# mLSTM mixing in a fused model block: column sums in four groups at once with a fold, and the mixing a half slot later

## What is computed

```python
scores = einsum('jd,sd->js', q, k) * w            # w: exp of gate sums, masked
den    = sum(scores, axis=-1)                     # "denominators"
out    = (scores @ v) / maximum(abs(den), exp(-m))
hh     = out[forward] + out[backward]
mu     = mean(hh, axis=-1)
var    = mean((hh - mu) ** 2, axis=-1)            # "variances"
y      = (hh - mu) * rsqrt(var + eps) * ln_w * sigmoid(o) ... * silu(z)
```

## Time and profile before

| what | us |
|---|---|
| median of 3 runs | 1283.39 (1282.34 to 1285.04) |
| the profiled execution, its own time | 1281.4 |
| its span, first to last instruction | 1279.6 |
| TensorE busy | 1204.3 |
| VectorE busy | 865.3 |
| ScalarE busy | 603.3 |
| GpSimd busy | 198.5 |

### The profile page before, as it was taken

One profiled execution on the slowest core, in us unless ns is written; L12 is line 12 of the kernel. 1 busy time (PEld: TensorE's weight loads), 2 busy tenths in 40 slices (PEclk: granted clock), 3 DMA queues, 4 the chain that ended last, 5 costly groups with the idle time before them and its releaser, 6 DMA issues.

```text
span 1279.6 us, 22795 instructions
## 1 busy us (share of the span) xinstructions
PE 1204.3 (94%) x9284; PEld 1118.9 (87%) x9284; DVE 865.3 (68%) x1355; ACT 603.3 (47%) x920; POOL 198.5 (16%) x145
## 2 busy tenths in 40 slices
PE   5799899999999999989999999999989789999996
PEld 2477698978888999989999899999978778999996
DVE  2889834458688867564368887665478996876644
ACT  3423354556656455651253354453455555445433
POOL 1334100000000000002000412210006951122000
PEclk9799999999999999999999999999999899999999
DMA  9565312214222355540345435545523213455550
GB/s 387 234 266 219 143 44 107 82 67 165 99 99 99 109 188 211 197 167 31 104 171 190 163 134 197 194 169 194 196 101 129 103 60 139 168 194 194 171 195 33
DMA packets 27475, 195.58 MB, mean 153 GB/s; under 512 B 3192, under 2 KB 3328, under 8 KB 3968
## 3 DMA queue, kind: packets, MB, share of 16 engines
q1 hardware_dynamic: 26496, 191.90, 41.5%
q10 hardware_dynamic: 896, 2.50, 0.5%
HBM read 193.33 MB, written 1.05 MB: 152 GB/s over the span
## 4 chain that ended last, share of the span: by engine, by line
PE 81%; DVE 10%; ACT 4%; issue 1%; DMA 0%; POOL 0%; ACTq 0%; DVEq 0%
PE ps L444 24%; PE ps L445 23%; PE ps L446 23%; DVE acc L2212 3%; PE ps L469 3%; PE ps L727 2%; DVE w_lo L1593 2%; PE ps L553 1%; PE ps L715 1%; PE ps L484 1%; DVE xconv L1697 1%; ACT w_hi L1010 1%; ACT x_hi L1306 1%; PE ps L612 1%; PE ps L777 1%
## 5 line engine op out<-in xcount | busy, mean ns | idle before, releaser
L1593 DVE TENSOR_TENSOR w_lo<-ring,w_hi 128x1024 fp32r<-128x1024 f32 x282 | 349.0, 1256 | 173.6 <-ACT w_hi L1010 166.6
L1010 ACT ACTIVATE w_hi<-ring 128x1024 fp32r<-128x1024 f32 x304 | 315.1, 1054 | 305.5 <-PE ps L446 220.5
L444 PE MATMUL ps<-x_hi,w_hi 128*128 128x258 f32 (+1 forms) x1216 | 346.5, 285 | 7.6 <-DVE x_lo L1943 4.1
L445 PE MATMUL ps<-x_lo,w_hi 128*128 128x258 f32 (+1 forms) x1216 | 344.0, 283 | 0.0
L446 PE MATMUL ps<-x_hi,w_lo 128*128 128x258 f32 (+1 forms) x1216 | 343.7, 283 | 0.0
L444 PEld LDWEIGHTS ps<-x_hi,w_hi 128*128 128x128 f32 x1216 | 231.0, 190 | 11.0 <-issue 10.8
L445 PEld LDWEIGHTS ps<-x_lo,w_hi 128*128 128x128 f32 x1216 | 231.1, 190 | 0.1
L446 PEld LDWEIGHTS ps<-x_hi,w_lo 128*128 128x128 f32 x1216 | 230.7, 190 | 0.0
L444 PE MATMUL ps<-g_hi,w_hi 128*128 128x256 f32 x608 | 171.0, 281 | 3.1 <-POOL g_lo L1537 1.7
L446 PE MATMUL ps<-g_hi,w_lo 128*128 128x256 f32 x608 | 170.3, 280 | 0.0
L445 PE MATMUL ps<-g_lo,w_hi 128*128 128x256 f32 x608 | 170.3, 280 | 0.0
(11 more groups left out here) (348 smaller groups left out, 1959.3 us busy)
## 6 DMA issues: line engine op xcount, KB each, us to landing
ring<-in_weights SPq DMA_DIRECT2D x156, 1024.0 KB, 4.8
o_sb<-in_weights SPq DMA_DIRECT2D x10, 1024.0 KB, 7.1
ada_room<-in_weights SPq DMA_DIRECT2D x10, 1024.0 KB, 7.0
V<-in_weights SPq DMA_DIRECT2D x3, 1024.0 KB, 22.6
dft<-in_dft ACTq DMA_DIRECT2D x1, 1026.0 KB, 7.0
X<-in_x SPq DMA_DIRECT2D x1, 1024.0 KB, 5.2
ctx_room<-in_ctx SPq DMA_DIRECT2D x1, 1024.0 KB, 7.6
xconv<-in_weights SPq DMA_DIRECT2D x1, 1024.0 KB, 28.0
```

Source lines behind the costliest of these rows:

```text
L444: mm(dst, w_h, x_h, start=start, stop=False, skip_group_check=True)
L445: mm(dst, w_h, x_l, start=False, stop=False, skip_group_check=True)
L1010: do(w_hi[:, q % 2, part], ring[:, q % RING, part], ACT.Copy).then_inc(S("hi_ready"), 1)
L1593: v.tensor_tensor(w_lo[:, q % 2, part], ring[:, q % RING, part], w_hi[:, q % 2, part], ALU.subtract).then_inc(S("lo_ready"), 1)
```

## The change

The sum of weights of a head (`denominators`) becomes four matmuls with 32 output rows each, one per tile t of source tokens, into four bands of partitions of the same bank. ScalarE copies the bank to `den_parts` (`move_den`), and behind the next half slot one matmul with all ones adds the bands (`fold_denominators`). The sum of squares (`head_var`) becomes four matmuls in bands likewise, a copy to `arow` (`move_var`) and a matmul `fold_var`, which stands behind the next head's `fold_denominators`, or for the last head behind half slot 35. Each band holds 32 equal rows, so the results are 32 times too large, and the readers divide by 32 (`scale` of the root, factors in `normalise`). `mix_values` and `head_mean` stand one half slot later, the next head's `spread` too. On ScalarE `root(n-1)` moves behind `next_slot(5 + 3n)`. On VectorE only the memset of `ones` moves, behind `finish_head(3)`.

```diff
             def denominators(hd):
                 pe.wait_ge(S("weighted_ready"), hd + 1)
                 w = wexp[hd % 2]
                 for t in range(4):
-                    last = mm(ps[:, 2, :], ones[:, :], w[:, :, t, :], start=(t == 0), stop=(t == 3))
-                last.then_inc(S("den_done"), 1)
+                    last = mm(ps[32 * t:32 * t + 32, 2, :], ones[:, 0:32], w[:, :, t, :], start=True, stop=True,
+                              skip_group_check=True)
+                last.then_inc(S("den_parts_done"), 1)
+
+            def fold_denominators(hd):
+                pe.wait_ge(S("den_parts_moved"), hd + 1)
+                mm(ps[:, 2, :], ones[:, :], den_parts[:, :, :], start=True, stop=True).then_inc(S("den_done"), 1)
...
             def head_var(hd):
                 pe.wait_ge(S("head_squares"), hd + 1)
-                column_sum(ps[:, 3, SEQ:2 * SEQ], ones_h[:, :], lambda k: work(3)[:, k, :], HC, None,
-                           S("head_var"))
+                for c in range(HC):
+                    last = mm(ps[32 * c:32 * c + 32, 3, SEQ:2 * SEQ], ones_h[:, 0:32], work(3)[:, c, :],
+                              start=True, stop=True, skip_group_check=True)
+                last.then_inc(S("var_parts_done"), 1)
+
+            def fold_var(hd):
+                pe.wait_ge(S("var_parts_moved"), hd + 1)
+                mm(ps[:, 3, SEQ:2 * SEQ], ones[:, :], arow[:, :], start=True, stop=True).then_inc(S("head_var"), 1)
...
             for n in range(HEADS):
                 at = 11 + 6 * n
                 denominators(n)
-                halves(at, at + 3)
+                halves(at, at + 1)
+                fold_denominators(n)
+                if n:
+                    fold_var(n - 1)
+                halves(at + 1, at + 4)
                 if n + 1 < HEADS:
                     spread(n + 1)
                 mix_values(n)
-                halves(at + 3, at + 4)
+                halves(at + 4, at + 5)
                 head_mean(n)
-                halves(at + 4, at + 6)
+                halves(at + 5, at + 6)
                 head_var(n)
-            halves(11 + 6 * HEADS, 2 * (N_OZ + N_MOUT))
+            at = 11 + 6 * HEADS
+            halves(at, at + 1)
+            fold_var(HEADS - 1)
+            halves(at + 1, 2 * (N_OZ + N_MOUT))
...
+            def move_den(hd):
+                act.wait_ge(S("den_parts_done"), hd + 1)
+                do(den_parts[:, :, :], ps[:, 2, :], ACT.Copy).then_inc(S("den_parts_moved"), 1)
+
+            def move_var(hd):
+                act.wait_ge(S("var_parts_done"), hd + 1)
+                do(arow[:, :], ps[:, 3, SEQ:2 * SEQ], ACT.Copy).then_inc(S("var_parts_moved"), 1)
...
             for n in range(HEADS):
+                move_den(n)
                 next_slot(5 + 3 * n)
+                if n:
+                    root(n - 1)
                 next_slot(6 + 3 * n)
                 if n + 1 < HEADS:
                     weigh(n + 1)
...
                 squares(n)
                 next_slot(7 + 3 * n)
-                root(n)
+                move_var(n)
             next_slot(N_OZ + 1)
+            root(HEADS - 1)
             round_y(HEADS - 1)
...
-                chain.step(v.scalar_tensor_tensor(r, den, -1.0, r, ALU.mult, ALU.max))
+                chain.step(v.scalar_tensor_tensor(r, den, -1.0 / 32, r, ALU.mult, ALU.max))
                 chain.join()
-                chain.step(v.tensor_tensor(r, den, r, ALU.max))
+                chain.step(v.scalar_tensor_tensor(r, den, 1.0 / 32, r, ALU.mult, ALU.max))
...
             lo(STARTS["mout"] + 3)
-            dve.wait_ge(S("den_done"), HEADS)
+            finish_head(HEADS - 1)
             v.memset(ones[:, :], 1.0 / 32).then_inc(S("ones_ready"), 1)
-            finish_head(HEADS - 1)
             rest_of_y(HEADS - 1)
```

More of the change, by code:

```diff
@@ L217, in program @@
                                             ("tail_lo", (P, SEQ), F32R))
-        silc, gate_and_tail, _ = one_place("gate_room", (P, 2, SEQ), ("silc", (P, KD, 62), F32),
+        silc, gate_and_tail, den_parts = one_place("den_parts", (P, 2, SEQ), ("silc", (P, KD, 62), F32),
                                            ("gate_and_tail", (P, 2, SEQ), F32R))
@@ L1230, in root @@
                     act.wait_ge(S("y_rounded"), hd)
-                do(rstd[:, 0:SEQ], ps[:, 3, SEQ:2 * SEQ], ACT.Sqrt, bias=eps[:, 0:1])\
+                do(rstd[:, 0:SEQ], ps[:, 3, SEQ:2 * SEQ], ACT.Sqrt, bias=eps[:, 0:1], scale=1.0 / 32)\
                     .then_inc(S("head_root"), 1)
```

## The result

The changed kernel takes 1296.99 us (median of five runs, 1296.03 to 1299.2) against 1283.04 us before (1281.9 to 1285.04): a ratio of 1.0107, interval 1.0091 to 1.0123, 14 us slower. The forecast was 1295.6 us. The profiled execution took 1299.2 us (span 1297.4), the slowest of the five, so its rows show some 2 us more than the median does.

What follows compares the result with a forecast made beforehand. TensorE's queue was taken to bound the stage. Work saved, waits and stage end, -8.2 + 15.05 + 0.9 = +7.8 us, plus 4.4 for the clock, gave +12.2 over 1283.4: 1295.6 us, range 1289.0 to 1299.3.

Steps and rivals of the forecast that it cites:

- the side: Whole kernel: the change makes it slower, chance 0.94, against 0.02 for the same and 0.04 for faster.
- The bound: Head-mixing stretch: TensorE is busy the whole window, 32.76 of 32.76 us, so its work and waits set the time.
- The matmul work, 8.2 us less: TensorE's sums: per head 5.16 us removed and 3.11 added, 2.05 less, 8.2 us less for four heads.
- The wait, 15.05 us: Half slot at+3: TensorE waits for the low part behind normalise, 4.1 us in head 0, 3.65 in heads 1 to 3.
- The mean, the squares and the copies: Mean to variances and ScalarE's copies: no cost, with 0.3 us in hand for the squares and 0.1 for the copies.
- third rival: ScalarE's copies come late, folds of heads 1 to 3 wait up to 0.6 us each: 1297.4 us, chance 0.14.
- The end of the stage, 0.9 us: Output projection's slot 4: finish_head(3) comes 1.3 us later, less 0.42 for the fold, 0.9 us more wait, bounds 0 and 2.
- The clock, 4.4 us: TensorE behind the four new waits: 3.4 falls of the granted clock at 1.3 us each, +4.4 us, upper bound 1.7 each.
- Total: Whole kernel: +7.8 us with the clock unchanged plus 4.4 for the clock, +12.2 us, forecast median 1295.6 us, chance 0.62.
- What I said the profile would show: Four TensorE waits of 3.6 to 4.1 us, PEclk below 1.0, heads 34 to 36 us, VectorE's denominator wait above 14.3.
- The first rival: The four TensorE waits come but do not lower the clock: 1291.2 us, chance 0.17.
- The second, faster: Half slot at+3 finds its low part ready, so only the saved work shows: 1275.2 us, chance 0.05.

Runs made afterwards that it cites:

- e5: e1 with the last o/z result moved ahead of the next high part's second half on ScalarE, head 2's root behind it: 1276.53 us, ratio 0.9942 to the kernel before.
- e1: Changed kernel with the first half of the low part of slot oz+7+3n made ahead of normalise(n) on VectorE: 1281.37 us, ratio 0.9989 to the kernel before.
- e7: e5 with head 3's products by z placed ahead of centre on VectorE: 1276.48 us, ratio 0.9941 to the kernel before.
- e2: Changed kernel with spread, mixing and mean back at their old places, groups and folds kept: 1282.29 us, ratio 0.9996 to the kernel before.
- e4: Kernel before with only spread, mixing and mean moved one half slot later, sums as before: 1289.36 us, ratio 1.006 to the kernel before.
- e3: Changed kernel with seven unused matmuls of 256 columns between half slots at+2 and at+3 of each head: 1290.86 us, ratio 1.0069 to the kernel before.
- e10: Changed kernel with three unused matmuls of 256 columns between half slots at+2 and at+3 of each head: 1293.56 us, ratio 1.0075 to the kernel before.
- e6: e2 with the sum of weights as before, only the variances summed in groups and folded: 1282.18 us, ratio 0.9989 to the kernel before.

## Why the prediction was right

The time (1295.6, measured 1296.99), the side and the range held. Step by step:

- *The bound.* TensorE's queue decides in this stage: every microsecond of wait and clock went into the time, and e5 shows the same for the saving.
- *The matmul work, 8.2 us less.* The account of the stage leaves 8.3; the stages of e1, e5 and e7 with their waits taken out give 8.6 to 9.0, that of e2 7.9, and all of them some 9 once 0.27 us for the end and restart at each wait are counted (see e5 and e7). So the saving was forecast some 0.9 us too small, and the five waits some 0.9 us too cheap (15.05 + 0.9 against 15.5 + 5 x 0.27 = 16.9); that these two cancel is luck. In head 1 the two groups, one behind the other, took 351.90 - 347.51 - 2.88 = 1.51 us where the sum had 1.83, which had let each group pay a start of its own. The folds took 0.86 and 0.43.
- *The wait, 15.05 us.* Measured 4.04 + 3.61 + 3.61 + 3.71 = 14.97. This is the term that decides the sign, and e1 shows its cause: take the low part from behind normalise, and those waits vanish. What I had not seen is the second reason at half slot 32, the bare move of the last o/z result; e1 and e4 laid it open.
- *The mean, the squares and the copies.* No wait there in any profile. The copy of the weights' parts of head 1 ended 0.2 us before the fold began (351.09 + 0.60 against 351.90), where I had worked out 0.1. The third rival did not happen, by that margin, and what the Trainium skill ("TensorEngine Tiling (Array Packing)", Performance Considerations) warns of, that the copy out of PSUM becomes the bottleneck, did not show here.
- *The end of the stage, 0.9 us.* Measured 0.56, and VectorE's list was its cause (e7). For the old sums (e4) the same 0.9 was expected and 0.2 came.
- *The clock, 4.4 us.* This term was mis-sized. I had 3.4 falls of 1.3 us; in the profile there were four, and they cost 8.3 us: 2.4, 2.8, 1.5 and 1.6. The price of 1.3 came from windows behind the stretch at 939 us, in which the clock was at its full level for part of the time; here two half slots ran at 0.50 from end to end, and a half slot at 0.50 costs 2.4. A row that I had shown, with 0.50 over the whole 2.0 us behind the 4.01 us stretch, pointed there, and I did not price by it. My upper bound of 1.7 per fall was too low as well. e3 shows that it is the clock, and that it hangs on the idle stretch. The four falls behind 3.6 to 4.0 us agree with the advice of the Trainium skill ("TensorE: Matmul & The Clock Gate", Why this matters for your kernels) against idle gaps between bursts; by it all four lose clock, which was nearer than my 3.4.
- *Total.* With the measured clock my sum would have been +16 us, against +15.5 in the stage of the profiled execution. The median rose by 14.0. So that the forecast of +12.2 over 1283.4 came within 1.4 us of the median is in part luck: the clock term was 3.9 us too small, and against the profiled execution, which the terms describe, the forecast was 1293.6 and the time 1299.2. The profiled execution is 2.2 us above its kernel's median, that of before 1.6 below, and these 3.8 us hid the error. About 2.3 us of the 17.8 between the spans lie outside the stage, 1.0 ahead of it and 1.3 behind. The fall of the clock at 286 us, present in this profile of the changed kernel and absent in that of the kernel before, is enough for the 1.0 ahead (the 72 matmuls behind that stretch take 10.28 us for 9.26). Behind the stage, too, the clock fell in one profile and not in the other: behind a stretch of 1.73 us at 754 us (737 us before) only in the changed kernel's, behind one of the same length at 1090 us (1070 us before) only in that of before. The same spread may be why e2's stage is 3.1 us shorter while its median moved by 1.3; how the clock falls in the executions that were not profiled stays open.
- *What I said the profile would show.* The four waits and the dips of PEclk are there. The heads are 36.7, 37.1 and 35.7 us long from one sum of weights to the next (forecast 34 to 36, before 32.8), because of the clock. VectorE's wait for the denominators did not grow: it shrank, and its waits for the spread and the mean grew instead. VectorE's waits from the first sum of weights to 475 us, to be read against the earlier trace rows:

```profile
DVE wexp L1858 <- PE ps L709: 18.1, 3, 6.6
DVE room L1886 <- PE ps L469: 12.9, 4, 7.6
DVE V L1872 <- PE ps L723: 7.4, 4, 2.7
```

and the one for the mean before:

```profile
DVE room L1851 <- PE ps L469: 5.5, 4, 3.3
```

VectorE is idle for longer in these groups (38 us against 14.3 and 5.5; before, it did not wait for the spread behind the first sum of weights), while TensorE waits for it: idle time on either side, and only the order between them at fault. The first rival (waits without a clock loss) is what e3 built by hand. The second, faster, is not what happened, but e5 reaches its 1275 us to within 1.5 us once the order is mended.

## What to carry to other kernels

When work is moved past the half slots of an in-order stream, list for each engine what stands behind the wait that the moved work feeds: here the next weights' low part stood behind the very chain that the mixing used to cover. Compare chain and cover in microseconds; a shortfall of 3.7 us ate a saving of 2 us per head. Where a wait on TensorE can't be avoided, price the clock behind it at the full loss of the work that follows at half rate, and look for the order that removes it: one half of `lo` moved ahead of the chain and one move on ScalarE turned 14 us lost into 7.7 us gained.

## What the runs showed of the hardware

- Useless matmuls in a wait made the kernel faster: with 12 us of them the median was 1290.86 us instead of 1296.99 (the stage 174.7 instead of 182.7), and TensorE kept the granted clock of 1.00.
- Idle stretches of 3.6 us and more lowered the clock each time in the stage (eight of eight in the two profiles of the changed kernel), one of 3.05 us did (e1), and one of 2.74; those of 2.31 to 2.42 us in e10 and of 2.38 us in e2 did not, and one of 2.25 us did in six of twelve profiles. Outside the stage the clock also fell behind shorter ones (places by the profile of the kernel before): behind 1.74 us at 737 us in seven of the twelve profiles, behind 1.73 us at 1070 us in five, behind 2.08 us at 987 us in all twelve, behind 1.70 us at 709 us in none. So at 1.7 to 2.3 us the length alone doesn't tell whether the clock falls.
- Two sums in column groups, one right behind the other, cost 1.51 us together (256 and 512 columns), and a group of 256 columns ahead of full-width matmuls 0.57 us (e6), against 0.45 us ahead of another group.
